# Dilated attention with the values stationary in column halves, outputs held features by tokens, group weights spread by a 0/1 product

## The reference, cut to what matters

```python
def dilated_attention_mixer(h, w_in, w_out, rel_table):
    z = h @ w_in
    qkv = z[..., :B_QKV].reshape(bsz, s, 3, 3, 16, 64)       # 3 groups, 16 heads of 64
    gate = z[..., B_QKV:]
    for gi, (window, dil) in enumerate(((128, 1), (512, 4), (2048, 16))):
        o, lse = dilated_window_group(q, k, v, table, dil, window // (2 * dil))
    wts = jax.nn.softmax(jnp.stack(lses), axis=0)            # one weight per group, token and head
    o = jnp.einsum('gbsh,gbshd->bshd', wts, jnp.stack(outs))
    y = o.reshape(bsz, s, B_WIDTH) * jax.nn.silu(gate)
    return y @ w_out
```

## Time and profile before

| | us |
|---|---|
| median of 3 runs | 2996.45 (2994.77 to 2997.16) |
| the profiled execution, its own time | 2994.64 |
| its span | 2992.8 |
| TensorE busy, of the span | 2941.7 |
| VectorE, ScalarE, GpSimd busy | 1225.8, 1050.0, 121.5 |

### The profile page before, as it was taken

How to read it: one execution, slowest core, us unless ns; L and a number is a source line. 1 busy time by engine, 2 the same in 40 slices (tenths; PEclk the granted TensorE clock), 3 DMA queues, 4 the chain that set the end, 5 groups by cost and what they waited for, 6 DMA issues and landing times.

```text
span 2992.8 us, 35944 instructions
## 1 busy us (share of the span) xinstructions
PE 2941.7 (98%) x15392; PEld 2470.8 (83%) x15392; DVE 1225.8 (41%) x1724; ACT 1050.0 (35%) x1747; POOL 121.5 (4%) x176
## 2 busy tenths in 40 slices
PE   7999999999999999999999999999999999999998
PEld 6888888888888888888868888898888886788887
DVE  4364253343333742333674333162322358633323
ACT  3323234344443332322473222132222248532221
POOL 1000000003000100000100000010000011000000
PEclk9999999999999999999999999999999999999999
DMA  5433222223222223323303222253232330223321
GB/s 194 140 99 99 99 99 85 85 66 105 78 78 71 92 85 99 99 99 113 88 16 109 93 94 99 99 157 99 86 100 96 101 97 2 71 85 99 99 99 71
DMA packets 145918, 279.89 MB, mean 94 GB/s; under 512 B 29818, under 2 KB 45354, under 8 KB 145632
## 3 DMA queue, kind: packets, MB, share of 16 engines
q1 hardware_dynamic: 136064, 247.17, 25.7%
q0 software_dynamic: 9696, 30.44, 3.3%
HBM read 271.17 MB, written 4.25 MB: 92 GB/s over the span
## 4 chain that ended last, share of the span: by engine, by line
PE 91%; DVE 4%; ACT 2%; issue 1%; DMA 1%; SPq 0%; POOL 0%; POOLq 0%; DVEq 0%; ACTq 0%
PE bank L594 25%; PE bank L596 25%; PE bank L595 25%; PE bank L753 2%; PE bank L732 2%; PE bank L605 2%; PE bank L608 2%; PE bank L607 2%; PE bank L819 1%; PE bank L787 1%; PE bank L803 1%; PE bank L741 1%; PE bank L713 1%; PE bank L1203 0%; PE bank L954 0%
## 5 line engine op out<-in xcount | busy, mean ns | idle before, releaser
L1675 DVE TENSOR_TENSOR w_low<-raw,w_high 128x2048 fp32r<-128x2048 f32 (+2 forms) x212 | 479.3, 2261 | 1187.0 <-ACT w_high L1305 1181.2
L594 PE MATMUL bank<-xt_high,w_high 128*128 128x512 f32 x1976 | 775.8, 393 | 1.3 <-DVE w_low L1675 0.8
L596 PE MATMUL bank<-xt_high,w_low 128*128 128x512 f32 x1976 | 769.8, 390 | 0.0
L595 PE MATMUL bank<-xt_low,w_high 128*128 128x512 f32 x1976 | 769.1, 389 | 0.0
L1305 ACT ACTIVATE w_high<-raw 128x2048 fp32r<-128x2048 f32 (+2 forms) x212 | 400.1, 1888 | 900.9 <-PE bank L596 895.4
L596 PEld LDWEIGHTS bank<-xt_high,w_low 128*128 128x128 f32 x1976 | 370.2, 187 | 79.3
L594 PEld LDWEIGHTS bank<-xt_high,w_high 128*128 128x128 f32 x1976 | 370.4, 187 | 78.3 <-DVE w_low L1675 1.3
L595 PEld LDWEIGHTS bank<-xt_low,w_high 128*128 128x128 f32 x1976 | 370.6, 188 | 75.5
L596 PE MATMUL bank<-w_high,hidden_low 128*128 128x512 f32 x640 | 249.0, 389 | 0.0
L594 PE MATMUL bank<-w_high,hidden_high 128*128 128x512 f32 x640 | 249.0, 389 | 0.0
L595 PE MATMUL bank<-w_low,hidden_high 128*128 128x512 f32 x640 | 249.0, 389 | 0.0
(11 more groups left out here) (360 smaller groups left out, 3899.9 us busy)
## 6 DMA issues: line engine op xcount, KB each, us to landing
raw<-in_ffn_w_gu SPq DMA_DIRECT2D x80, 1024.0 KB, 5.2
raw<-in_ffn_w_down SPq DMA_DIRECT2D x44, 1024.0 KB, 5.0
raw<-in_b_w_in SPq DMA_DIRECT2D x40, 1024.0 KB, 5.2
raw<-in_a_w_in SPq DMA_DIRECT2D x24, 1024.0 KB, 5.2
raw<-in_a_w_out SPq DMA_DIRECT2D x8, 1024.0 KB, 4.9
raw<-in_ffn_w_gu SPq DMA_DIRECT2D x16, 512.0 KB, 4.6
raw<-in_w_out SPq DMA_DIRECT2D x5, 1024.0 KB, 4.9
raw<-in_w_mem_kv SPq DMA_DIRECT2D x4, 1024.0 KB, 5.3
```

Source lines behind the costliest of these rows:

```text
L594: pe.matmul(o, lh, rh, start=start, stop=False, skip_group_check=True)
L595: pe.matmul(o, lh, rl, start=False, stop=False, skip_group_check=True)
L596: return pe.matmul(o, ll, rh, start=False, stop=stop, skip_group_check=True)
L1675: dve.tensor_tensor(homes[n][1][:, 0:w], RAW[n % 2][:, 0:w], homes[n][0][:, 0:w].bitcast(F32), ALU.subtract).then_inc(sem["w_low_ready"], ...
```

## The change

- **Values** (`attend_slot` on TensorE). 64 columns of `b_v_rows` are stationary and the 128 queries of `b_pt` move. Task s - 5 writes partitions 0 to 63 of `bank7`, task s - 4 partitions 64 to 127, and the two take turns. The bank then holds features by tokens. VectorE copies both tasks' outputs at once, `[P, n * 128]`, into `b_o` `[P, 8, 512]`, features by tokens in natural order (for groups 1 and 2 with a stride of 4).
- **Reordering.** Only the maxima and sums of group 0 are still reordered, 32 DMAs.
- **Group weights.** VectorE writes them padded to 32 columns a group (`b_weights_padded`); TensorE turns them (`turn_weights`, 4 transposes), ScalarE copies them to `b_weights_t` (row 32 g + h, columns tokens in natural order). `spread_weights(j)` multiplies, for each group, 32 rows of the constant `b_spread` (row h has ones at the 64 features of head h) by `b_weights_t`: three float32 products of 512 columns into banks 4, 5, 6, which hold each group's weight for 128 features and all tokens. `b_spread` is a new input of 96 by 1024, loaded over GpSimd's queue.
- **Merge.** For each block j of 128 features: three products with the banks, two sums, the gate, all on VectorE; ScalarE writes `b_y_high` and VectorE `b_y_low` from `b_o0`. The 32 transposes of `turn_half` and GpSimd's 8 products are gone.
- **Gate.** The gate's product gives features by tokens.
- **Panels.** b_out's panel 2 has a ring buffer; its panel 3 and the next layer's first two gate panels keep places of their own, and now wait for b_out's panel 0 to be used (`freed_by`).

Below, "..." also stands for the lines that are taken out from `turn_half` on; they are in the listing above.

```diff
+    bO = [at_off(f"b_o{g}", [P, KD, SEQ], rg + a * KB) for g, a in enumerate((40, 24, 56))]
...
+    bG = at_off("b_gate", [P, KD, SEQ], rg)
+    bYH = at_off("b_y_high", [P, KD, SEQ], rg + 24 * KB, F32R)
+    bYL = at_off("b_y_low", [P, KD, SEQ], rg + 56 * KB, F32R)
+    SPREAD = at_off("b_spread", [96, D], r0)
+    bWT = at_off("b_weights_t", [96, SEQ], r0 + 4 * KB)
+    bWP = at_off("b_weights_padded", [P, TT, 3, 32], r0 + 6 * KB)
...
-    EDGES = {"s1": ("a_out", (0, 8), ("b", 0, 0, "q"), (64, 72, 80, 32)),
+    EDGES = {"s2": ("b_out", (16, 72), ("gate", 0, 0, 0), (0, 8, 80, 40)),
...
-    for i, (g, high, low) in enumerate(zip(ids["b_out"][2:] + ids["gate", 0, 0, 0], (72, 48, 0, 24), (80, 64, 8, 32))):
-        home(f"s2_{i}", g, high, low)
...
-                        va.append((e * 64, [(P, (e * 2 + w) * P, bV[:, (b + w) % TT, h * 64:h * 64 + 64])
-                                            for w in range(2)]))
+                        va += [(s, e, (e * 2 + w) * P, bV[:, (b + w) % TT, h * 64:h * 64 + 64], w == 0, w == 1)
+                               for w in range(2)]
...
-                                    ("copy", heads_of(bON, b, g0, 2), 128),
+                                    (bO[0][:, x0:x0 + 2, P * b:P * b + P], 2),
...
-                                ("copy", heads_of(bO[g], r, g0, 4), 256),
+                                (bO[g][:, 4 * hf:4 * hf + 4, r:SEQ:4], 4),
@@ -745,14 +744,13 @@
...
                     pe.wait_ge(sem["o_read"], at("o_read", (name, s - 6)))
-                for m in (s - 5, s - 4):
-                    pe.wait_ge(sem["pt_copied"], at("pt_copied", (name, m)))
-                    for c, parts in tasks[m]["values"]:
-                        o = 256 * (m % 2) + c
-                        for i, (K, a, v) in enumerate(parts):
-                            ins = pe.matmul(ps[7][:, o:o + 64], PTs[m % 4][0:K, a:a + P], v,
-                                            start=i == 0, stop=i == len(parts) - 1)
-                    ins.then_inc(sem["weighted"], step("weighted", (name, m)))
+                pe.wait_ge(sem["pt_copied"], at("pt_copied", (name, s - 4)))
+                for i in range(4):
+                    for m in (s - 5, s - 4):
+                        half, x, a, v, start, stop = tasks[m]["values"][i]
+                        ins = pe.matmul(ps[7][half:half + 64, x * P:x * P + P], v, PTs[m % 4][:, a:a + P], start=start, stop=stop)
+                        if i == 3:
+                            ins.then_inc(sem["weighted"], step("weighted", (name, m)))
         def product_beside(name, jobs, free, beside):
@@ -824,17 +822,27 @@
                 if behind:
                     behind(u)
...
+        def turn_weights():
+            pe.wait_ge(sem["group_weights"], at("group_weights"))
+            pe.wait_ge(sem["o_read"], at("o_read", (("b", 2, 1), 7)))
+            for r in range(TT):
+                ins = pe.transpose(ps[7][0:96, r * P:r * P + P], bWP[:, r].rearrange("p g h -> p (g h)"), ident[:])
+            ins.then_inc(sem["weights_turned"], step("weights_turned"))
+        def spread_weights(j):
+            if j == 0:
+                pe.wait_ge(sem["spread_loaded"], at("spread_loaded"))
+                pe.wait_ge(sem["weights_spread"], at("weights_spread"))
+            else:
+                pe.wait_ge(sem["spread_used"], at("spread_used", j - 1))
+            for g in range(3):
+                q = slice(32 * g, 32 * g + 32)
+                ins = pe.matmul(ps[4 + g][:], SPREAD[q, j * P:j * P + P], bWT[q, :], start=True, stop=True)
+                ins.then_inc(sem["spread_done"], step("spread_done", (j, g)))
         def b_out_product():
@@ -845,31 +853,32 @@
...
             for i in range(2):
                 pe.wait_ge(sem["w_low_ready"], at("w_low_ready", gs[i]))
+                pe.wait_ge(sem["b_split"], at("b_split", 2 * i + 1))
                 for t in (0, 1):
                     if i == 0:
                         pe.wait_ge(sem["bgate_read"], at("bgate_read", (1, 2 * t + 1)))
                     accumulate(t, i, i == 0, False)
...
+                    if (i, t) in ((0, 1), (1, 0)):
+                        spread_weights(6 + i)
             for i in range(2):
                 for t in (2, 3):
...
+                    if i == 0 and t == 2:
+                        pe.wait_ge(sem["spread_used"], at("spread_used", KD - 1))
                     ins = accumulate(t, i, i == 0, False)
                 ins.then_inc(sem["product_done"], step("product_done", ("panel", gs[i])))
             for t, i in ((0, 2), (0, 3), (1, 2), (1, 3), (2, 2), (2, 3), (3, 2), (3, 3)):
                 if t < 2:
                     pe.wait_ge(sem["w_low_ready"], at("w_low_ready", gs[i]))
+                    pe.wait_ge(sem["b_split"], at("b_split", 2 * i + 1))
                 ins = accumulate(t, i, False, i == 3)
                 if t >= 2 and i == 2:
@@ -994,18 +1003,20 @@
...
                            lambda slot: attend_slot(("b", *prev), 16 + slot))
             prev = f
...
+        gate_jobs = [(ps[j][:], feature(512, j * P, XTH, XTL)) for j in range(4)]
         def two_steps(slot):
             for s in (2 * slot, 2 * slot + 1):
                 attend_slot(("b", 2, 1), s)
...
+        def spread_beside(slot):
+            if slot == 0:
+                turn_weights()
+            if slot in (1, 2, 3, 5, 6, 7):
+                spread_weights((1, 2, 3, 5, 6, 7).index(slot))
         product_beside(("b_gate", 0), gate_jobs, lambda j: pe.wait_ge(sem["bv_read"], at("bv_read", (2, 1, j))), two_steps)
@@ -1516,25 +1527,28 @@
...
+            act.activation(bG[:, j, :], ps[j][:], ACT.Silu).then_inc(sem["bgate_read"], step("bgate_read", (0, j)))
         prepare(ids["b_gate", 0][1] + 2)
...
+        act.wait_ge(sem["weights_turned"], at("weights_turned"))
+        act.activation(bWT[:].rearrange("p (n r) -> p r n", r=TT), ps[7][0:96, :].rearrange("p (r n) -> p r n", r=TT),
+                       ACT.Copy).then_inc(sem["weights_spread"], step("weights_spread"))
+        def high(j):
+            act.wait_ge(sem["y_gated"], at("y_gated", j))
+            act.activation(bYH[:, j, :], bO[0][:, j, :], ACT.Copy).then_inc(sem["b_high"], step("b_high", j))
+        high(0)
+        high(1)
         prepare(ids["b_gate", 1][0] + 2)
...
+        high(2)
+        for j in range(4):
+            act.wait_ge(sem["product_done"], at("product_done", ("acc", ("b_gate", 1), j)))
+            act.activation(bG[:, 4 + j, :], ps[j][:], ACT.Silu).then_inc(sem["bgate_read"], step("bgate_read", (1, j)))
+            if j < 2:
+                high(3 + j)
         prepare(ids["b_gate", 1][1] + 2)
...
+        for j in range(5, KD):
+            high(j)
         rows("s2", "b_out")
@@ -1824,13 +1838,11 @@
...
+                dve.wait_ge(sem["weighted"], at("weighted", (name, s - 5)))
                 dve.wait_ge(sem["weighted"], at("weighted", (name, s - 4)))
...
+                dst, n = tasks[s - 4]["finish"]
+                dve.tensor_copy(dst, ps[7][:, 0:n * P].rearrange("p (x n) -> p x n", x=n)).then_inc(
+                    sem["o_read"], step("o_read", (name, s - 5), (name, s - 4)))
@@ -1967,6 +1979,8 @@
...
         dve.wait_ge(sem["maxed"], at("maxed", (last, len(ATT[last][0]) - 1)))
+        dve.wait_ge(sem["o0_permuted"], at("o0_permuted"))
+        dve.memset(bWP[:].rearrange("p t g h -> p (t g h)"), 0.0)
@@ -1980,55 +1994,42 @@
...
         ins.then_inc(sem["group_weights"], step("group_weights"))
         attend_slot(last, 11)
...
         dve.wait_ge(sem["o_read"], at("o_read", (last, len(ATT[last][0]) - 1)))
...
+        def merge(j):
+            for g in range(3):
+                dve.wait_ge(sem["spread_done"], at("spread_done", (j, g)))
+                ins = dve.tensor_tensor(bO[g][:, j, :], bO[g][:, j, :], ps[4 + g][:], ALU.mult)
+            ins.then_inc(sem["spread_used"], step("spread_used", j))
+            dve.wait_ge(sem["spread_used"], at("spread_used", j))
+            link(dve.tensor_tensor(bO[0][:, j, :], bO[0][:, j, :], bO[1][:, j, :], ALU.add))
+            dve.tensor_tensor(bO[0][:, j, :], bO[0][:, j, :], bO[2][:, j, :],
+                              ALU.add).then_inc(sem["merged_rows"], step("merged_rows", j))
+        def gate(j):
+            dve.wait_ge(sem["merged_rows"], at("merged_rows", j))
+            dve.wait_ge(sem["bgate_read"], at("bgate_read", (j // 4, j % 4)))
+            dve.tensor_tensor(bO[0][:, j, :], bO[0][:, j, :], bG[:, j, :], ALU.mult).then_inc(sem["y_gated"], step("y_gated", j))
+        def low(j):
+            dve.wait_ge(sem["b_high"], at("b_high", j))
+            dve.tensor_tensor(bYL[:, j, :], bO[0][:, j, :], bYH[:, j, :].bitcast(F32),
+                              ALU.subtract).then_inc(sem["b_split"], step("b_split", j))
+        prepare(ids["b_gate", 0][1] + 2)
+        merge(0)
+        gate(0)
+        for j in range(1, KD):
+            merge(j)
+            if j in (3, 5):
```

(7 more changed lines are left out.)

115 lines of the change are left out of this document (13 added, 102 removed).

## The result

The changed kernel takes 2975.87 us (median, 2975.74 to 2975.91), the kernel before 2996.25 us beside it (2994.77 to 2997.16): 20.4 us less, ratio 0.9924 with a 95% interval of 0.9905 to 0.9944. The forecast was 2979 us. In the later comparisons 10 of 59 runs of the kernel before, three of seven of E1 and three of twelve of E4 took 10 to 14 us more than the rest, at a mean granted clock of 0.993 or 0.994 instead of 0.996 or more, while none of the 79 runs of the changed kernel, its variants and E12 did; no trace shows why, and since they are in the ratios, E1 and E4 are read by their profiled executions.

What follows compares the result with a forecast made beforehand. TensorE, busy for 98% of the span, was taken to bound the kernel. Values -21.5 us and the stage +4.1 us sum to -17.4: profiled 2994.64 becomes 2977.2, the median 2979 us; range 2972 to 2991.

Steps and rivals of the forecast that it cites:

- The values: Attention on TensorE: 32 blocks of values shrink from 1.71 to 1.03 us each, a gain of 21.5 us.
- The drain: Tiling-mode changes at the values' blocks drain TensorE; counted as 0.17 us a block, without it the gain would be 27 us.
- The rival that the halves don't overlap: Values' column halves don't overlap: 1.98 us a block against 1.9, 3003 us in all; chance 0.04.
- Spreads: Stage after attention: three products in different row groups run side by side, 1.26 us a set, 10.1 us for 8.
- rival B: Spreads' three row groups don't run side by side, a set costs some 1.6 us more: 2989 us; chance 0.17.
- The waits: Merge stage and next layer's start: 8.4 us of TensorE's waits go, new ones of 3.7 and 2.2 us come.
- rival C: VectorE keeps up in the merge and the row tile is in time; most of 5.9 us falls away: 2974 us; chance 0.12.
- The stage: Spreads, merge and output product: 12.5 us leave and 16.6 us come in, a net cost of 4.1 us.
- The clock: Merge stage: granted clock at 1.00 throughout, the half-clock stretch and its 2.4 us gone, no new wait long enough.
- Removed work priced at nothing: Attention and merge: output copies, group 0's reordering DMAs and GpSimd's eight products held up nobody, so 0 us.
- F: Values get shorter but attention slots don't, as weights or exponentials become late: half the gain, 2990 us; chance 0.04.

Runs made afterwards that it cites:

- E1: Kernel before with only the values' products changed to the new form; median 2978.02 us, ratio 0.9957, profiled execution 2976.78 us.
- E4: Kernel before with VectorE making b_out's first low panel earlier, ahead of two merges; 2995.73 us, ratio 1.0.
- E12: Kernel before with VectorE making both of b_out's first two low panels earlier; 2991.80 us, ratio 0.9986.
- E9: Changed kernel with the values' block ahead of the transposes in odd steps; 2972.37 us, ratio 0.9921.
- E2: Changed kernel with all four values' products of one task, then all four of the other, instead of turns; 2993.67 us, ratio 0.9987.
- E3: Changed kernel with all three spreading products of a set reading rows 0 to 31; 2992.83 us, ratio 0.9984.
- E10: Changed kernel with TensorE waiting before the output product for b_split of block 4 instead of block 1; 2985.49 us, ratio 0.9961.
- E11: Changed kernel with 16 DMAs like the removed reordering of group 0's outputs put back; 2977.66 us, ratio 0.9938.

## Why the prediction was right, point by point

- **The values** (forecast 0.67 to 0.68 a block, 21.5 us). The block's own length was exact, 1.03 us. The mis-sized term is the entry: I counted the change of shape once, inside the block, and took the 0.44 us from the transposes to the block as given. It is 0.52 now, and 0.32 instead of 0.23 behind an ordinary product; 32 times 0.09 is 3.0 us. The exit grows by 0.02. So a block gives 0.57 us, and the values 18.3 (E1), 3.2 less than forecast. The stretch as a whole gives 19.5; the other 1.2 are the gate's product, below.
- **Why the old form was slow.** The forecast doesn't say. Its instructions stand 0.11 us apart though only 64 columns move. Its weight loads, of 128 columns each, fill 60.1 of its 60.7 us; those of the new form, of 64 columns, 27.3 of 35.0. That the loads set the old pace is argued from this, not shown.
- **The drain.** The Trainium skill (TensorEngine Tiling (Array Packing), Key Properties) says that a change of tiling mode drains the engine. The trace agrees in so far as each change costs time, and gives sizes: 0.09 us into a block that was not there before, behind transposes and behind ordinary products alike, beside the 0.17 inside it. E9 doesn't get the 0.09 back. That these pauses are the drain is argued from where they lie.
- **The rival that the halves don't overlap** (E). The values take 35.0 us and not 60. E2 shows that all of it is overlap: with four of eight instructions of a task beside the other's 0.19 us a block is saved, with turns 0.67. The rival's price, 1.98 us a block, was too high even for halves one behind the other (1.51).
- **Spreads** (forecast 1.26 us a set). Measured 1.25, three together, and 2.77 a set for the products alone when they share rows (E3), which is rival B's price a set for a case that did not come; B had left out the clock, which fell three times.
- **The waits** (forecast 5.9 us). 3.9 came, in the places named: 1.66 at set 5 (1.75), 1.64 at the first `x_rows` (2.2), 0.2 for the Silu (0.6), 0.4 before rows 2 and 3 (0.7); the 0.2 for a panel and 0.4 for set 7 did not come. VectorE's block is 4.45 us and not 4.6, over eight blocks 1.2 us, which can be most of the difference: rival C's mechanism, in part. The 2.2 us also hold a slip: 12.5 us leave ahead of the `x_rows` and 14.4 come in, so TensorE gets there at about 1061.2 on before's clock and not 1060.7, and the wait comes out at 1.6.
- **The stage** (forecast +4.1 us). Measured +1.5. 2.0 of the difference are these waits. The rest is a thing I had not counted: with features on the partitions of the bank the gate's product moves `xt` past stationary weights, and its instructions start some 0.227 us apart where before they were 0.235 (988.15 to 988.37 and the like), 0.8 us for the 96 of a half. The same holds for the gate's first half, beside the attention's last unit: with the four shorter exits it is the 1.2 us that E1 lacks.
- **The clock.** At 1.00 throughout, as forecast, with no wait over 1.7 us; E10 shows the price otherwise. The forecast feared waits over 3 us; in E12 a stretch at 0.67 stands behind one of 2.6, so shorter ones are not safe.
- **Removed work priced at nothing** (reordering, copies, GpSimd's products). No wait in the trace is tied to them; E11 finds none for the reordering in its stretch; the others were not tried by themselves. The slots did not stay long for other reasons either (F): the `b_pt` waits are 3.1 us before and after.

By the profiled executions the gain was 1.5 us larger than forecast. Errors of opposite sign cancelled in part: the gain by the values was put 3.2 us too high, the waits 2.0 us too high, and some 2.0 us from the gate's product were not counted (1.2 in its first half, 0.8 in its second). 0.2 us lie ahead of the attention and 0.8 behind the stage. The mechanism of the values is the forecast one; that the sum came so near is partly luck.
